# Placing stores, norm transfers and convolution tails two to four tiles later or earlier around a DeltaNet input projection

## The chip, the cores and the metric

The kernel runs on one core of one Trainium2 chip, in one launch. The metric is device time in microseconds (us); lower is better. Three runs of the kernel before gave 3073.43, 3074.57 and 3079.75 us, a median of 3074.57.

## What is computed

One inference step of a two-layer decoder for 512 prompt tokens and 8 x 4 sampled tokens, 544 in all, which share the weights. Each layer is half a feed-forward block, a token mixer, and half a feed-forward block. Layer 0 mixes by causal pooling, layer 1 by a gated DeltaNet. The change lies in the input projection of that DeltaNet:

```python
proj = h @ w_in                        # 1024 -> q, k (8 heads each), v, z (16 each), b and a
qkv, new_conv = short_conv(qkv_raw, conv_past, conv_w)   # 4 taps, then silu; also the last 3 rows
q = l2norm(q); k = l2norm(k)
o, s_new = chunk_gated_delta(q, k, v, beta, g, s0)
o = rmsnorm(o, norm_w) * silu(z)
```

`new_conv`, the last three rows before the convolution for the prompt and for each of the 8 sampled sequences, is an output of its own.

## The kernel before

All engines are programmed by hand; each runs its own list in order, and semaphores join them. Weights come in **tiles** of 128 output columns (1024 x 128, 512 KB), in two slots that take turns. For each tile SyncE (SP) issues the load into `wraw` (L400), ScalarE (ACT) rounds it into `whi` (L1039), GpSimd (POOL) makes the rest `wlo` (L545), and TensorE (PE) does 48 matmuls (L681) into one of two accumulators `acc`. SP may load a slot when POOL has read it (`w_lo`); ACT may round into a slot when PE has finished the tile two before (`acc_done`).

The input projection, `delta_in` on each engine, has 49 tiles, j = 0 to 48, written as one Python loop over j per engine: tile 0 holds b and a, tiles 1 to 16 q and k, 17 to 32 v (`V0` = 17), 33 to 48 z (`Z0` = 33). For q, k and v VectorE (DVE) scales the result into `ub` and, one tile later, adds three taps (L1653); ACT does the first tap (L1124) and the silu (L1136, L1137). A z tile is scaled by DVE (L1695) and goes through silu on ACT (L1158). The results of v and z stand in four buffers `sv` that take turns: SP stores each one to scratch memory (L452, L460 for the last two) and ACT waits for the store of four tiles before (`vz_stored`). When q and k are through (`SS_UNIT` = 18), ACT makes the inverse norms `rs16` in its iteration 19 (L1147, L1150); SP sends them to memory (L443), and reads them back spread over all partitions into `y`, four heads at a time (`norms`, L436, 1088 KB each). DVE multiplies them in, two heads per z tile (`key_norm`, L1659), and SP stores those heads (L457). Where these transfers stand between the loads is set in the SP loop by numbers alone:

```python
for j in range(IN_UNITS + 2):
    fill(j)                                  # load of tile j; 49 and 50 are the first two of w_out
    if j == SS_UNIT + 3:
        sp.wait_ge(nq_rs, 2)
        sp.dma_start(rs_d, rs16[:, 1, :]).then_inc(rs_out, 16)
...
    n = j - V0 - 4
    if 0 <= n < HV + ZT:
        sp.wait_ge(vz_silu, n + 1)
```

The convolution's rows (`tailc`) are turned by PE in eight groups of four transposes (L980), one after each tile from `TAIL_UNIT` = 41 on, and copied by DVE to `crow` (L1707, L1709). SP stores them as nine small transfers of three rows (L462, L464). The stage that follows, `delta_core`, lies over the same memory: DVE waits for all stores (`qk_stored`, `vz_stored`, `conv_stored`), clears `Y`, `S` and `gate` (L1488 to L1491), and by the last of these allows SP to load the first chunk (L491), for which PE waits (L763).

Of the kernel before, what the change touches and what calls it, by code (L numbers as in the profile page):

```python
# [8 lines left out]
SEQ, NB, NS = 512, 8, 4  # L9
# [4 lines left out]
HK, HV, DK = 8, 16, 128  # L14
CONV_DIM = 2 * HK * DK + HV * DK
CT = CONV_DIM // P
ZT = HV
CW = 4
# [21 lines left out]
CTAIL = CW - 1 + NB * NS  # L40
# [23 lines left out]
def cols(hf):  # L64
    return slice(hf * HT, (hf + 1) * HT)
# [16 lines left out]
def build(nc, consts, I, O):  # L82
# [5 lines left out]
    with ctx:  # L88
        def sb(name, shape, dt=F, scope=ctx):
            return scope.enter_context(nc.sbuf_tensor(name, shape, dt))  # L90

        def sem(name):
            return ctx.enter_context(nc.semaphore(name))
# [37 lines left out]
        aux = [ctx.enter_context(nc.psum_tensor(f"aux{b}", [P, 512], F)) for b in range(4)]  # L131
# [40 lines left out]
        vz_silu = sem("vz_silu")  # L172
        vz_stored = [sem(f"vz_stored{s}") for s in range(4)]
# [11 lines left out]
        tail_ps = sem("tail_ps")  # L185
        crow_c = sem("crow_c")
        gates_ready = sem("gates_ready")
        conv_stored = sem("conv_stored")
# [133 lines left out]
        with ExitStack() as sc:  # L322
# [4 lines left out]
            sv = [sb(f"sv{s}", [P, T], F, sc) for s in range(4)]  # L327
            sqn = sv[2:4]
            tailc = sb("tailc", [P, CT, CTAIL], F, sc)
            crow = sb("crow", [CTAIL, CONV_DIM], F, sc)  # L330
# [21 lines left out]
        v_d = nc.dram_tensor("v_scratch", [HV, P, T], F, kind="Internal").ap()  # L352
        z_d = nc.dram_tensor("z_scratch", [HV, P, T], F, kind="Internal").ap()
# [12 lines left out]
        def in_unit(j):  # L366

            return IN_BASE + j, slot(IN_BASE + j), visit(IN_BASE + j)
# [4 lines left out]

        Q0, V0, Z0 = 1, 1 + 2 * HK, 1 + CT
        SS_UNIT = Q0 + 2 * HK + 1
        TAIL_UNIT = Z0 + 8

        block = ctx.enter_context(nc.Block())

# [2 lines left out]
        def _(sp):  # L382
# [13 lines left out]
            def load(unit, i, src, nk, width=P):  # L396

                s, v = slot(unit), visit(unit)
                sp.wait_ge(w_lo[s], i + (v + 1))
                sp.dma_start(wraw[s][:, 0:nk, 0:width], src.rearrange("(k p) n -> p k n", p=P))\  # L400
                  .then_inc(raw_full[s], 16)
# [17 lines left out]
            def load_out(i, k):  # L419
                load(OUT_BASE + k, i, w_out[k * D:(k + 1) * D, bass.ds(i * P, P)] if not isinstance(i, int)  # L420
                     else w_out[k * D:(k + 1) * D, i * P:(i + 1) * P], KT)

            def delta_in():
                def fill(j):
                    if j == 0:
                        load(IN_BASE, 0, w_in[:, (CT + ZT) * P:(CT + ZT) * P + 2 * HV], KT, 2 * HV)
                    elif j < IN_UNITS:
                        load(IN_BASE + j, 0, w_in[:, (j - 1) * P:j * P], KT)
                    else:
                        load_out(0, j - IN_UNITS)  # L430

                def norms(b):
                    sp.wait_ge(rs_out, 16)
                    if b >= 2:
                        sp.wait_ge(nq_done, 4 * (b - 1))
                    sp.dma_start(y[:, 4 * (b % 2):4 * (b % 2) + 4, :], rs_d[4 * b:4 * b + 4, :].partition_broadcast(P))\  # L436
                      .then_inc(rs_in[b % 2], 16)

                for j in range(IN_UNITS + 2):
                    fill(j)  # L440
                    if j == SS_UNIT + 3:
                        sp.wait_ge(nq_rs, 2)
                        sp.dma_start(rs_d, rs16[:, 1, :]).then_inc(rs_out, 16)  # L443
                    if j == SS_UNIT + 4:
                        norms(0)
                        norms(1)
                    if j in (Z0 + 4, Z0 + 6):
                        norms((j - Z0) // 2)
                    n = j - V0 - 4
                    if 0 <= n < HV + ZT:  # L450
                        sp.wait_ge(vz_silu, n + 1)
                        sp.dma_start((v_d if n < HV else z_d)[n % HV], sv[n % 4][:, :]).then_inc(vz_stored[n % 4], 16)  # L452
                    n = j - Z0 - 3
                    if 0 <= n < HK:
                        sp.wait_ge(nq_done, 2 * n + 2)
                        for t in (2 * n, 2 * n + 1):
                            sp.dma_start(qk_d[t], qk[:, t, :]).then_inc(qk_stored, 16)  # L457
                for n in range(HV + ZT - 2, HV + ZT):
                    sp.wait_ge(vz_silu, n + 1)
                    sp.dma_start(z_d[n % HV], sv[n % 4][:, :]).then_inc(vz_stored[n % 4], 16)  # L460
                sp.wait_ge(crow_c, 8)
                sp.dma_start(O["conv_prompt"][0, 0, :, :], crow[0:CW - 1, :]).then_inc(conv_stored, 16)  # L462
                for b in range(NB):
                    sp.dma_start(O["conv_sample"][0, b, :, :], crow[CW - 1 + NS * b + 1:CW - 1 + NS * (b + 1), :])\  # L464
                      .then_inc(conv_stored, 16)
                sp.wait_ge(conv_stored, 16 * (NB + 1))

            def load_sampled(i, q):
# [201 lines left out]
        def _(pe):  # L670
# [272 lines left out]
            def delta_in():  # L943
                pre(4)
                ready = lambda hf: (h_lo, 16 * NTH[4] + 8 * (hf + 1))
                for j in range(IN_UNITS):
# [17 lines left out]
                    if 0 <= t < 2 * HK:  # L964
# [6 lines left out]
                        last.then_inc(nq_ss, 1)  # L971
                    b = j - TAIL_UNIT
                    if 0 <= b < 8:
# [318 lines left out]
        def _(dve):  # L1292
            def take(u, i, hf):

                s, v = slot(u), visit(u)
                dve.wait_ge(acc_done[s], (i + v) * 2 + hf + 1)
                return acc[s][:, hf, 0:HT]
# [86 lines left out]
            for t, n in TT:  # L1384
                for kk in range(2):
                    b = 2 * t + kk
# [216 lines left out]
            def delta_in():  # L1603
                b, a = bat[:, :, 0:HV], bat[:, :, HV:2 * HV]
# [63 lines left out]
                for j in range(IN_UNITS):  # L1668
                    u, s, v = in_unit(j)
                    if j == 0:  # L1670
                        for hf in range(2):
                            bank = take(u, 0, hf)
                            dve.tensor_tensor(ba[:, cols(hf)], bank[0:2 * HV, :], rpre[0:2 * HV, hf, :], ALU.mult).then_inc(taken[s], 1)
                    elif j < Z0:
                        c = j - Q0
                        dst = ub[c % 2]
                        samp = dst[:, CW - 1 + SEQ:UB].rearrange("p (b t) -> p b t", b=NB)
                        if c >= 2:
                            dve.wait_ge(conv_done, 3 * (c - 1))
                        dve.tensor_copy(samp[:, :, 0:CW - 1], pastc[:, c, :].rearrange("p (b t) -> p b t", b=NB))  # L1680
                        dve.tensor_tensor(dst[:, CW - 1:CW - 1 + HT], take(u, 0, 0), rpre[:, 0, :], ALU.mult).then_inc(taken[s], 1)
                        bank = take(u, 0, 1)
                        n = SEQ - HT
                        dve.tensor_tensor(dst[:, CW - 1 + HT:CW - 1 + SEQ], bank[:, 0:n], rpre[:, 1, 0:n], ALU.mult)
                        dve.tensor_tensor(samp[:, :, CW - 1:CW - 1 + NS], samples(bank[:, n:HT], 0), samples(rpre[:, 1, n:HT], 0),
                                          ALU.mult).then_inc(taken[s], 1)
                    else:
                        z = j - Z0
                        dst = conv[z % 2]
                        if z < 2:  # L1690
                            dve.wait_ge(vz_silu, HV - 1 + z) if z else dve.wait_ge(vz_silu, HV - 1)
                        else:
                            dve.wait_ge(vz_silu, HV + z - 1)
                        for hf in range(2):
                            last = dve.tensor_tensor(dst[:, cols(hf)], take(u, 0, hf), rpre[:, hf, :], ALU.mult).then_inc(taken[s], 1)  # L1695
                    if 0 <= j - Q0 - 1 < CT:
                        taps(j - Q0 - 1)
                    for m, step in ((1, gates_1), (2, gates_2), (4, gates_3), (SS_UNIT + 1, gates_4)):
                        if j == m:
                            step()  # L1700
                    if Z0 + 1 <= j <= Z0 + HK:
                        for t in range(2 * (j - Z0 - 1), 2 * (j - Z0)):
                            key_norm(t)
                    bb = j - TAIL_UNIT - 1
                    if 0 <= bb < 7:
                        dve.wait_ge(tail_ps, bb + 1)
                        dve.tensor_copy(crow[:, bb * 512:(bb + 1) * 512], aux[3 - bb % 2][0:CTAIL, :]).then_inc(crow_c, 1)  # L1707
                dve.wait_ge(tail_ps, 8)
                dve.tensor_copy(crow[:, 7 * 512:8 * 512], aux[2][0:CTAIL, :]).then_inc(crow_c, 1)  # L1709

            def pool_mixer():
                dve.memset(hp[:, :, 0:POOLP], 0.0).then_inc(hp_ready, 1)
# [81 lines left out]
            for t, n in TT:  # L1794
                for kk in range(2):
                    b = 2 * t + kk
# [56 lines left out]
```

## Time and profile before

| | |
|---|---|
| three runs | 3073.43, 3074.57, 3079.75 us |
| the profiled execution's own time | 3073.24 us |
| its span | 3071.5 us |
| mean granted TensorE clock | 0.919 of full speed |
| PE busy | 2699.7 us, 88% of the span |
| DVE, POOL, ACT busy | 1223.3, 968.3, 831.1 us |

The span runs from the first to the last instruction of the profiled execution; some 1.7 us lie around it. `delta_in` fills about 1404 to 1755 us of it, and the first matmul of `delta_core` starts at 1779.76. Matmul times in the rows are from start to a modelled end and overlap, so that the pace is read from starts and counts.

### The profile page before, as it was taken

To read this page: it belongs to the slowest core of one execution; us is meant where nothing else is said; L and a number is where in the kernel's file an instruction comes from. 1 tells how busy PE (TensorE), PEld (TensorE's weight loads), DVE (VectorE), ACT (ScalarE), POOL (GpSimd) and SP (SyncE) were. 2 spreads that over 40 slices of the span, in tenths; PEclk is the share of its full clock that TensorE was granted. 3 is DMA by queue.
4 is the path that set the end of the run, shared out by engine and by line. 5 is a ranking of instruction groups with operands and counts; after the bars stand their busy time and mean duration, and the time that the engine had idled before them with its cause. 6 is when DMAs were issued, how large, how long until landed. Compare 5 with 4: busy or idle time off the path is not lost.

```text
span 3071.5 us, 51275 instructions
## 1 busy us (share of the span) xinstructions
PE 2699.7 (88%) x20143; PEld 2580.1 (84%) x20143; DVE 1223.3 (40%) x2204; ACT 831.1 (27%) x1296; POOL 968.3 (32%) x453
## 2 busy tenths in 40 slices
PE   7999974899998999997989878989866649899997
PEld 7999972899997999996889868888754349799996
DVE  4313328531334322327776255454422342531334
ACT  4422221431323422224443211011100042441321
POOL 2333322233342333432333323132111323233432
PEclk9999987999999999998999989999955579999998
DMA  3332320132331232231246410010024323132231
GB/s 108 89 89 82 92 71 19 57 93 78 89 91 53 86 96 78 84 88 42 76 126 180 148 49 21 20 41 20 27 61 113 115 79 89 55 91 86 82 95 57
DMA packets 424267, 239.39 MB, mean 78 GB/s; under 512 B 15462, under 2 KB 411983, under 8 KB 423622
## 3 DMA queue, kind: packets, MB, share of 16 engines
q1 hardware_dynamic: 413523, 233.37, 26.0%
q10 hardware_dynamic: 10670, 5.01, 0.6%
q8 instruction: 50, 0.82, 0.1%
q14 instruction: 24, 0.20, 0.0%
HBM read 208.18 MB, written 30.52 MB: 78 GB/s over the span
## 4 chain that ended last, share of the span: by engine, by line
PE 81%; DVE 9%; DMA 3%; ACT 2%; SPq 2%; issue 1%; POOL 1%; DVEq 0%; ACTq 0%; POOLq 0%
PE acc L681 64%; PE aux L802 2%; PE aux L813 1%; PE acc L813 1%; PE acc L802 1%; DVE y L1323 1%; PE aux L817 1%; PE acc L817 1%; DVE x L1326 1%; PE aux L690 1%; PE acc L880 1%; PE aux L880 1%; DVE rpost L1301 1%; PE acc L908 1%; DMA wraw<-in_dn_w_in_dram 1%
## 5 line engine op out<-in xcount | busy, mean ns | idle before, releaser
L545 POOL TENSOR_TENSOR wlo<-wraw,whi 128x1024 fp32r<-128x1024 f32 (+2 forms) x305 | 784.8, 2574 | 1434.5 <-ACT whi L1039 1434.5
L681 PE MATMUL acc<-hhi,whi 128*128 128x272 f32 x3600 | 1042.4, 290 | 13.1 <-POOL wlo L545 13.1
L681 PE MATMUL acc<-hlo,whi 128*128 128x272 f32 x3600 | 1044.6, 290 | 0.0
L681 PE MATMUL acc<-hhi,wlo 128*128 128x272 f32 x3600 | 1037.3, 288 | 0.0
L681 PEld LDWEIGHTS acc<-hhi,whi 128*128 128x128 f32 x3600 | 678.8, 189 | 21.5 <-POOL wlo L545 13.8
L681 PEld LDWEIGHTS acc<-hhi,wlo 128*128 128x128 f32 x3600 | 679.6, 189 | 0.5
L681 PEld LDWEIGHTS acc<-hlo,whi 128*128 128x128 f32 x3600 | 677.5, 188 | 0.3
L1039 ACT ACTIVATE whi<-wraw 128x1024 fp32r<-128x1024 f32 (+2 forms) x305 | 340.0, 1115 | 407.1 <-PE acc L681 327.7
L681 PE MATMUL acc<-hidhi,whi 128*128 128x272 f32 x1408 | 406.2, 289 | 12.4 <-DVE hidlo L1348 12.4
L681 PE MATMUL acc<-hidhi,wlo 128*128 128x272 f32 x1408 | 407.6, 290 | 0.0
L681 PE MATMUL acc<-hidlo,whi 128*128 128x272 f32 x1408 | 405.0, 288 | 0.0
L681 PEld LDWEIGHTS acc<-hidhi,whi 128*128 128x128 f32 x1408 | 265.5, 189 | 14.1 <-issue 14.1
L681 PEld LDWEIGHTS acc<-hidlo,whi 128*128 128x128 f32 x1408 | 265.0, 188 | 0.0
L681 PEld LDWEIGHTS acc<-hidhi,wlo 128*128 128x128 f32 x1408 | 264.8, 188 | 0.0
L1341 DVE TENSOR_TENSOR tmpu<-acc,rpre 128x272 f32<-128x272 f32 x176 | 77.7, 441 | 344.0 <-PE acc L681 344.0
L1339 DVE TENSOR_TENSOR tmpg<-acc,rpre 128x272 f32<-128x272 f32 x176 | 77.7, 441 | 309.1 <-PE acc L681 308.1
L1080 ACT ACTIVATE hidhi<-hidf 128x272 f32 (+1 forms) x176 | 76.0, 432 | 418.9 <-DVE hidf L1345 418.9
L1345 DVE TENSOR_TENSOR hidf<-tmpu,sil 128x272 f32<-128x272 f32 x176 | 145.9, 829 | 6.0
L1653 DVE SCALAR_TENSOR_TENSOR conv<-ub,convw,conv 128x568 f32<-128x568 f32 x96 | 140.4, 1462 | 5.6 <-ACT conv L1124 3.3
L1076 ACT ACTIVATE sil<-tmpg 128x272 f32<-128x272 f32 x176 | 75.7, 431 | 225.0 <-DVE tmpg L1339 224.5
L1360 DVE COPY y<-acc 128x272 f32 x64 | 28.3, 441 | 238.9 <-PE acc L681 238.9
L1060 ACT ACTIVATE sqt<-y 128x272 f32 (+1 forms) x96 | 41.3, 431 | 296.8 <-DVE y L1362 199.2
(309 smaller groups left out, 3082.3 us busy)
## 6 DMA issues: line engine op xcount, KB each, us to landing
wraw<-in_w_ffn_gate_dram SPq DMA_DIRECT2D x88, 512.0 KB, 3.8
wraw<-in_w_ffn_up_dram SPq DMA_DIRECT2D x88, 512.0 KB, 3.8
wraw<-in_w_ffn_down_dram SPq DMA_DIRECT2D x64, 704.0 KB, 4.5
wraw<-in_dn_w_in_dram SPq DMA_DIRECT2D x48, 512.0 KB, 4.1
wraw<-in_dn_w_out_dram SPq DMA_DIRECT2D x16, 512.0 KB, 4.0
Ss<-in_state_delta_dram SPq DMA_DIRECT2D x16, 512.0 KB, 6.7
out_delta_sample_dram<-Ss SPq DMA_DIRECT2D x16, 512.0 KB, 5.9
v_scratch<-sv SPq DMA_DIRECT2D x16, 272.0 KB, 2.2
```

The lines of the kernel that those rows point to most:

```text
L545: pool.tensor_tensor(wlo[s][:, 0:nk, 0:width], wraw[s][:, 0:nk, 0:width], whi[s][:, 0:nk, 0:width].bitcast(F), ALU.subtract).then_inc(w_lo ...
L681: last = pe.matmul(acc[s][0:width, hf, 0:HT], w[s][:, k, 0:width], a[:, k0 + k, cols(hf)], start=(n == 0), stop=(n == 3 * nk - 1))
L802: last = pe.matmul(b0[0:r, heads(g, r // 2, h)].rearrange("p (b l) -> p b l", l=2 << lv), g.low[0:r, h, :], halves(g.U[0:r, h, :], lv)[:, ...
L813: last = pe.matmul(b1[0:r, heads(g, r // 2, h)].rearrange("p (b l) -> p b l", l=2 << lv), g.T[0:r, h, :], halves(g.Y[lv][0:r, h, :], lv)[: ...
L817: last = pe.matmul(b1[0:r, heads(g, r // 2, 4 + h)].rearrange("p (b l) -> p b l", l=2 << lv), g.Y[lv][0:r, h, :], halves(g.T[0:r, h, :], l ...
L1039: act.activation(whi[s][:, 0:nk, 0:width], wraw[s][:, 0:nk, 0:width], ACT.Copy).then_inc(w_hi[s], 1)
L1076: act.activation(sil[:, hf, :], tmpg[:, hf, :], ACT.Silu).then_inc(gate_silu, 1)
L1080: act.activation(hidhi[:, bass.ds(i, 1), cols(hf)], hidf[:, hf:hf + 1, :], ACT.Copy).then_inc(hid_hi, 1)
L1339: dve.tensor_tensor(tmpg[:, hf, :], take(base, i, hf), rpre[:, hf, :], ALU.mult).then_inc(taken[sg], 1)
L1341: dve.tensor_tensor(tmpu[:, hf, :], take(base + 1, i, hf), rpre[:, hf, :], ALU.mult)\
L1345: dve.tensor_tensor(hidf[:, hf, :], tmpu[:, hf, :], sil[:, hf, :], ALU.mult).then_inc(hid_ready, 1)
L1653: dve.scalar_tensor_tensor(dst[:, 0:UB - 3], src[:, k:UB - 3 + k], convw[:, CT * k + c:CT * k + c + 1], dst[:, 0:UB - 3], ALU.mult, ALU.ad ...
```

## The change

In SP's loop the store of v or z tile n moves from j = V0 + n + 4 to V0 + n + 6; the norms' store from j = 21 to 24; the first two transfers back from 22 to 26, the others from 37 and 39 to 40 and 42; the q/k stores begin at j = 39 instead of 36. The last four z stores, not two, stand behind the loop. PE's tail transposes and DVE's copies begin at tile 34 (`TAIL_UNIT` = Z0 + 1) instead of 41, so that the last copy stands in the loop too, and the nine convolution stores are issued at j = 47, in front of the loads of tiles 48 to 50. No operation is added or taken away.

```diff
-        TAIL_UNIT = Z0 + 8
+        TAIL_UNIT = Z0 + 1
...
+                def store_vz(n):
+                    sp.wait_ge(vz_silu, n + 1)
+                    sp.dma_start((v_d if n < HV else z_d)[n % HV], sv[n % 4][:, :]).then_inc(vz_stored[n % 4], 16)
...
-                    if j == SS_UNIT + 3:
+                    if j == SS_UNIT + 6:
                         sp.wait_ge(nq_rs, 2)
                         sp.dma_start(rs_d, rs16[:, 1, :]).then_inc(rs_out, 16)
-                    if j == SS_UNIT + 4:
+                    if j == SS_UNIT + 8:
                         norms(0)
                         norms(1)
-                    if j in (Z0 + 4, Z0 + 6):
-                        norms((j - Z0) // 2)
-                    n = j - V0 - 4
+                    if j in (Z0 + 7, Z0 + 9):
+                        norms((j - Z0 - 3) // 2)
+                    n = j - V0 - 6
                     if 0 <= n < HV + ZT:
-                        sp.wait_ge(vz_silu, n + 1)
-                        sp.dma_start((v_d if n < HV else z_d)[n % HV], sv[n % 4][:, :]).then_inc(vz_stored[n % 4], 16)
-                    n = j - Z0 - 3
+                        store_vz(n)
+                    n = j - Z0 - 6
...
-                sp.wait_ge(crow_c, 8)
-                sp.dma_start(O["conv_prompt"][0, 0, :, :], crow[0:CW - 1, :]).then_inc(conv_stored, 16)
...
+                    if j == TAIL_UNIT + 13:
+                        sp.wait_ge(crow_c, 8)
+                        sp.dma_start(O["conv_prompt"][0, 0, :, :], crow[0:CW - 1, :]).then_inc(conv_stored, 16)
...
+                for n in range(HV + ZT - 4, HV + ZT):
+                    store_vz(n)
                 sp.wait_ge(conv_stored, 16 * (NB + 1))
```

SP's queue where the v tiles begin, before; the first row is the load of tile 21, and the wait in brackets is what SP must have before it issues the row:

```order
L400 DMA wraw<-in_dn_w_in_dram 128x8x128 [waits w_lo1]
L443 DMA rs_scratch<-rs 16x544 [waits nq_rs]
L452 DMA v_scratch<-sv 128x544 [waits vz_silu]
L400 DMA wraw<-in_dn_w_in_dram 128x8x128 [waits w_lo0]
L436 DMA y<-rs_scratch 128x2176 [waits rs_out] x2
L452 DMA v_scratch<-sv 128x544 [waits vz_silu]
```

And now, from the load of tile 24 to behind that of tile 26:

```order
L400 DMA wraw<-in_dn_w_in_dram 128x8x128 [waits w_lo0]
L447 DMA rs_scratch<-rs 16x544 [waits nq_rs]
L434 DMA v_scratch<-sv 128x544 [waits vz_silu]
L400 DMA wraw<-in_dn_w_in_dram 128x8x128 [waits w_lo1]
L434 DMA v_scratch<-sv 128x544 [waits vz_silu]
L400 DMA wraw<-in_dn_w_in_dram 128x8x128 [waits w_lo0]
L440 DMA y<-rs_scratch 128x2176 [waits rs_out] x2
L434 DMA v_scratch<-sv 128x544 [waits vz_silu]
```

The norms' store has moved behind three more loads, and the two transfers of the norms behind four more.

SP's queue where `delta_in` ends, before; the first row is the load of tile 48:

```order
L400 DMA wraw<-in_dn_w_in_dram 128x8x128 [waits w_lo0]
L452 DMA z_scratch<-sv 128x544 [waits vz_silu]
L400 DMA wraw<-in_dn_w_out_dram 128x8x128 [waits w_lo1]
L452 DMA z_scratch<-sv 128x544 [waits vz_silu]
L400 DMA wraw<-in_dn_w_out_dram 128x8x128 [waits w_lo0]
L452 DMA z_scratch<-sv 128x544 [waits vz_silu]
L460 DMA z_scratch<-sv 128x544 [waits vz_silu] x2
L462 DMA out_conv_prompt_dram<-crow 3x4096 [waits crow_c]
L464 DMA out_conv_sample_dram<-crow 3x4096 x8
L483 UNCONDITIONAL_BRANCH [waits vz_stored1,vz_stored2,vz_stored0,vz_stored3,qk_stored,conv_stored]
```

And now, from the load of tile 47:

```order
L400 DMA wraw<-in_dn_w_in_dram 128x8x128 [waits w_lo1]
L434 DMA z_scratch<-sv 128x544 [waits vz_silu]
L463 DMA out_conv_prompt_dram<-crow 3x4096 [waits crow_c]
L465 DMA out_conv_sample_dram<-crow 3x4096 x8
L400 DMA wraw<-in_dn_w_in_dram 128x8x128 [waits w_lo0]
L434 DMA z_scratch<-sv 128x544 [waits vz_silu]
L400 DMA wraw<-in_dn_w_out_dram 128x8x128 [waits w_lo1]
L434 DMA z_scratch<-sv 128x544 [waits vz_silu]
L400 DMA wraw<-in_dn_w_out_dram 128x8x128 [waits w_lo0]
L434 DMA z_scratch<-sv 128x544 [waits vz_silu] x5
L486 UNCONDITIONAL_BRANCH [waits vz_stored1,vz_stored2,vz_stored0,vz_stored3,qk_stored,conv_stored]
```

The nine convolution stores have moved from the end of the queue to in front of the load of the last z tile, and five z stores stand behind the last load.

## Rows read from the trace of the kernel before

**Rows 1.** The page, share of the chain that ended last, by engine.

```profile
PE 81%; DVE 9%; DMA 3%; ACT 2%; SPq 2%; issue 1%; POOL 1%; DVEq 0%; ACTq 0%; POOLq 0%
```

**Rows 2.** Busy time by stretch: PE, PEld, DVE, ACT, POOL, then PEclk, DMA, GB/s.

```profile
1600.00:1620.00 20.00, 20.00 (x162) 20.00 (x161) 18.34 (x23) 8.06 (x18) 8.19 (x4) 1.00 0.48 137
...
1680.00:1700.00 20.00, 19.22 (x135) 19.22 (x136) 4.74 (x9) 4.82 (x6) 8.20 (x4) 0.86 0.72 226
...
1759.00:1761.00 2.00, 0.00 (x0) 0.00 (x0) 0.00 (x0) 0.00 (x0) 0.00 (x0) 0.50 0.13 33
```

**Rows 3.** The chain that ended last, in order of time: start, us, what.

```profile
1550.80 6.24 PE acc L681 x48
...
1570.29 11.13 DMA wraw<-in_dn_w_in_dram
1582.59 2.40 POOL wlo L545
1585.03 78.80 PE acc L681 x624
...
1680.78 26.59 PE acc L681 x192
1707.37 0.44 PE aux L980 x4
...
1762.31 4.07 DMA out_conv_sample_dram<-crow
```

**Rows 4.** Timeline of PE: start, us, what, [idle before <- releaser].

```profile
1576.72 0.59 PE L681 MATMUL acc<-hhi,whi 128*128 128x272 f32 x1 [7.62 <-POOL wlo L545]
...
1680.78 0.60 PE L681 MATMUL acc<-hhi,whi 128*128 128x272 f32 x1 [4.89 <-POOL wlo L545]
...
1779.76 1.22 PE L763 MATMUL acc<-kT 128*128 128x128 f32 x4 [26.64 <-DMA vT<-v_scratch]
```

**Rows 5.** What SP's queue waited for, 1390 to 1800: us, times, longest.

```profile
SPq L443 <- ACT rs L1150: 20.5, 1, 20.5
SPq L457 <- DVE qk L1659: 20.4, 5, 7.0
...
SPq L491 <- DVE gate L1491: 8.7, 1, 8.7
```

**Rows 6.** Timeline of ACT in its iterations 19 and 20.

```profile
1557.12 1.06 ACT L1039 ACTIVATE whi<-wraw 128x1024 fp32r<-128x1024 f32 x1 [1.48 <-PE acc L681]
...
1566.36 0.66 ACT L1150 ACTIVATE rs<-rs 16x544 f32<-16x544 f32 x1
...
1567.09 0.25 ACT L1153 ACTIVATE gtmp<-gates 128x80 f32<-128x80 f32 x1
1573.19 1.06 ACT L1039 ACTIVATE whi<-wraw 128x1024 fp32r<-128x1024 f32 x1 [5.85 <-DMA wraw<-in_dn_w_in_dram]
```

**Rows 7.** Timeline of DVE: two sets of taps, and the first clearing.

```profile
1557.48 4.62 DVE L1653 SCALAR_TENSOR_TENSOR conv<-ub,convw,conv 128x568 f32<-128x568 f32 x3
...
1568.38 2.49 DVE L1653 SCALAR_TENSOR_TENSOR conv<-ub,convw,conv 128x568 f32<-128x568 f32 x3
...
1766.64 6.43 DVE L1488 MEMSET Y<- 128x512 f32 x12 [12.28 <-DMA out_conv_sample_dram<-crow]
```

**Rows 8.** Timeline of POOL: the split of tile 22, and the idle time before it.

```profile
1574.32 2.34 POOL L545 TENSOR_TENSOR wlo<-wraw,whi 128x1024 fp32r<-128x1024 f32 x1 [13.67 <-ACT whi L1039]
```

**Rows 9.** Line L460, the last two z stores: issue ns, starts; time to landing.

```profile
L460 SPq DMA_DIRECT2D z_scratch<-sv x2: 319/319/319, 1747.9 to 1754.4; - x2
...
DMA to landing us min/median/max: 2.0/2.0/2.0
```

**Rows 10.** Line L452, the other stores of v and z: time to landing.

```profile
DMA to landing us min/median/max: 2.0/4.5/10.4
```

**Rows 11.** The page, DMA issues: KB each, median us to landing.

```profile
wraw<-in_dn_w_in_dram SPq DMA_DIRECT2D x48, 512.0 KB, 4.1
```

**Rows 12.** Timeline of SP: the eight convolution stores of the samples.

```profile
1755.13 7.75 SPq L464 DMA_DIRECT2D out_conv_sample_dram<-crow x8
```

More of the change, by code:

```diff
@@ L457, in delta_in @@
                             sp.dma_start(qk_d[t], qk[:, t, :]).then_inc(qk_stored, 16)
-                for n in range(HV + ZT - 2, HV + ZT):
-                    sp.wait_ge(vz_silu, n + 1)
-                    sp.dma_start(z_d[n % HV], sv[n % 4][:, :]).then_inc(vz_stored[n % 4], 16)
-                sp.wait_ge(crow_c, 8)
-                sp.dma_start(O["conv_prompt"][0, 0, :, :], crow[0:CW - 1, :]).then_inc(conv_stored, 16)
-                for b in range(NB):
-                    sp.dma_start(O["conv_sample"][0, b, :, :], crow[CW - 1 + NS * b + 1:CW - 1 + NS * (b + 1), :])\
-                      .then_inc(conv_stored, 16)
+                    if j == TAIL_UNIT + 13:
+                        sp.wait_ge(crow_c, 8)
+                        sp.dma_start(O["conv_prompt"][0, 0, :, :], crow[0:CW - 1, :]).then_inc(conv_stored, 16)
+                        for b in range(NB):
+                            sp.dma_start(O["conv_sample"][0, b, :, :], crow[CW - 1 + NS * b + 1:CW - 1 + NS * (b + 1), :])\
+                              .then_inc(conv_stored, 16)
+                for n in range(HV + ZT - 4, HV + ZT):
+                    store_vz(n)
                 sp.wait_ge(conv_stored, 16 * (NB + 1))
@@ L1704, in delta_in @@
                     bb = j - TAIL_UNIT - 1
-                    if 0 <= bb < 7:
+                    if 0 <= bb < 8:
                         dve.wait_ge(tail_ps, bb + 1)
                         dve.tensor_copy(crow[:, bb * 512:(bb + 1) * 512], aux[3 - bb % 2][0:CTAIL, :]).then_inc(crow_c, 1)
-                dve.wait_ge(tail_ps, 8)
-                dve.tensor_copy(crow[:, 7 * 512:8 * 512], aux[2][0:CTAIL, :]).then_inc(crow_c, 1)
             def pool_mixer():
```

## The prediction

> **What bounds the kernel now.** I read the chain that ended last first: 81% of it is on TensorE [rows 1], so time is won only where PE stands still or runs slowly. The stretches of `delta_in` say where. From 1600 to 1620 PE issues 162 matmuls in 20 us at full clock [rows 2], and the chain shows the pace behind that: tiles 23 to 35, 624 matmuls, in 78.80 us, which is 6.06 us a tile [rows 3]. Nothing moved by the change can beat that pace. So I looked for PE's gaps, and its timeline has three: 7.62, 4.89 and 26.64 us [rows 4]. Behind each gap stands SP's queue. SP waited 20.5 us in one piece for the norms (L443) and 20.4 us in five for `key_norm` (L457) [rows 5]. While SP waits, the loads behind it in its list are not issued.
>
> *First gap.* The norms are ready at 1566.36 + 0.66 = 1567.0 [rows 6]. SP, which has issued tile 21, waits until then and only then loads tile 22. ACT was free at 1567.34 but gets the weights at 1573.19 [rows 6]. The load of tile 23 stands behind two 1088 KB transfers and takes 11.13 us [rows 3]. PE had ended tile 21 at 1576.72 - 7.62 = 1569.10 [rows 4]. At 6.06 a tile it would have begun tile 23 at 1575.1 and begins it at 1585.03 [rows 3]: 9.9 us lost.
>
> *Second gap.* Tiles 38 to 41 take 26.59 us instead of 24.24 [rows 3]; the mean granted clock is 0.86 from 1680 to 1700 [rows 2], so some of them ran at the lower of its levels, 1.2 GHz. With the gap of 4.89 [rows 4] that is 7.2 us lost.
>
> *Third gap.* PE ends at 1753.12. The last z store is issued at 1754.4 and lands 2.0 us later [rows 9]. But DVE starts to clear at 1766.64, released by the convolution stores, which are issued over 7.75 us behind it [rows 7, 12], the last landing 4.07 us after its issue [rows 3]. SP waits 8.7 us for DVE's clearing [rows 5], then come the loads.
>
> **The change, part by part.**
>
> *Norms and v stores later.* At j = 24 SP has the slot of tile 24 only after POOL has split tile 22, which is after ACT's norms, so the wait is empty. Tiles 22 and 23 are loaded in time. What remains is ACT's own lateness: it is busy until 1567.34, rounds tile 22 in 1.06 us [rows 6], POOL splits in 2.40 [rows 3], and with 0.1 between them PE starts at 1570.9, 1.8 us late. Then DVE's taps for the next silu run beside that split. Taps that ran beside a split took 4.62 us, and those at 1568.38, when POOL had been idle since 1560.65, took 2.49 [rows 7, 8]. With 4.62 the silu ends near 1573.9, tile 23 is split by 1577.4, and PE, which would want it at 1576.9, loses 0.5 more. In the Trainium skill, SBUF — State Buffer, section "SBUF: two separate sides", a VectorE operation with two SBUF inputs and a GpSimd one that reads SBUF exclude each other; the trace agrees (4.62 against 2.49), and without that exclusion the rest would be 1.8 instead of 2.3 us. I take 2.3: a gain of 9.9 - 2.3 = **7.6**. It can't pass 8.1, since ACT isn't free sooner; if ACT needs two more tiles to catch up at 1.3 each, it is 5.
>
> *Norms, z stores and q/k stores later.* The q/k store at j needs `key_norm` of tile j - 5, while SP arrives when POOL has split tile j - 2, which needs the end of tile j - 4 on PE. The waits of L457 (and of the norms in front) are then empty, and loads go out 3.6 us after PE ends a tile (1.06 + 2.40 and 0.1), two tiles ahead of need. Gain **7.2**; at worst 0, if bytes and not waits hold the loads. The slowest load seen, 11.13 us behind twice as many norms, would still land 14.8 us after that tile's end; rounding and splitting need 3.6 more, and PE needs the result at 18.2. So I expect none of the 7.2 to stay. DVE may wait a little for the third norm transfer; PE asks for that only a tile later.
>
> *Tails earlier.* Eight groups of transposes of 0.44 us [rows 3] stand in PE's list as before. Seven lay between tiles, the eighth behind the last; now all lie between: **0.4** lost. DVE is busy 4.74 of 20 us in that stretch [rows 2] and hides the copies; beyond that cover, PE would wait for `crow`.
>
> *Convolution stores earlier.* Their cost moves into SP's queue at j = 47. SP gets there 3.6 us after PE ends tile 43, issues the load and a z store (about 0.8), then the nine for 8.1. The load of tile 48 goes out 12.5 us after that end instead of 9.7. It must have landed by 18.2 + 2.5 = 20.7 (2.5 is what splitting in 3.6 leaves of a tile), 8.2 us after issue. These stores keep few DMA engines busy, 0.13 of 16, or two [rows 2], so the load's shares on those queue up. A load lands in 4.1 us in the median [rows 11]; I add 2 for that queue and take **0**. With the 11.13 us of the worst load it would be 2.9 late, and the lower clock would add some 2.4 as in the second gap: 5.
>
> In the Trainium skill, DMA: Bandwidth & Descriptors, section "Why a DMA increments its semaphore by 16 and not by 1", a transfer is spread over as many engines, up to 16, as divide the slowest dimension: three for rows of 3 x 4096, the lowest-numbered each time. The trace's 0.13 agrees with two or three. This speaks against the new place, since a weight load uses all 16 and lands with its slowest share.
>
> *End.* With the convolution stores done, DVE waits for the last z store: 1754.4 + 2.0 and the same 0.25 that lay between landing and clearing before, 1756.65 instead of 1766.64: **10.0** gained. The clearing and the first loads follow unchanged, and PE's clock, down at 0.50 (1.2 GHz) from 1759 to 1761 [rows 2], is down at either time. If that store landed only after 10.4, the slowest of L452 [rows 10], the gain would be 1.6.
>
> *Sum.* 7.6 + 7.2 - 0.4 - 0 + 10.0 = 24.4 us off the profiled execution's own 3073.24: 3048.8. It lies 1.3 below the median of the runs shown; I say **3049**. The terms' bounds give 5 to 8.1, 0 to 7.2, -5 to 0 and 1.6 to 10.0.
>
> **Rivals.**
>
> *The stores at j = 47 hold up the last tile.* For it: few engines, and the load behind them. Against it: 8.2 us of room. Price 5: **3054**.
>
> *The last store lands late.* Five z stores now stand behind the last loads. Against it: four of them have time to drain while PE works on tile 48, and the two of L460 landed in 2.0 [rows 9]. Price 8.4: **3057**.
>
> *The gaps only move.* If bytes, not SP's waits, starve the loads, both gaps come back where the norms stand now, and only the end is won: **3063**. The 11.13 us load speaks for it, the 20.5 us in which SP issued nothing speak against it. Were the end's gain gone too, nothing would be left: about 3073.
>
> *Slower: the ring of four `sv` buffers.* A z store is now issued about 4.4 us after the end of the second tile following, and ACT needs it 1.1 us after the end of the fourth: 8.8 us to land. ACT is busy 4.82 of 20 us [rows 2], 1.5 a tile, so 4.5 more are spare, and splitting has 2.5: PE stalls once stores take 15.8 us. To be slower by 6 it must lose 30.5 over 16 tiles, 1.9 each, that is 17.7 us a store; at 18 it would be 35 - 24.4 above before: **3084**. L452's landings, 4.5 median and 10.4 at worst [rows 10], are far from it.
>
> **How the numbers follow.** My forecast, 3044 to 3055 with its own bounds: 0.73. Last tile held up 0.08, last store late 0.06, gaps only move 0.06, nothing left 0.03, ring 0.04. A measurement of this kernel can tell 0.2%, 6.1 us, from no change. All but the last two are faster by more than that: 0.93; same 0.03; slower 0.04. The range 3043 to 3059 takes in the forecast and the first two rivals, 0.87 together, with 1 us below and 2 above.
>
> **What would show it.** In the profile after, SP's waits for the norms' store and for `key_norm` should be near nothing. PE's gap at the start of v should be 1.8 us and one of about 0.5 behind it, with the clock up; no gap between tiles 33 and 48; the convolution stores' issue should end before the last tiles, and DVE's clearing should be released by a z store, about 4 us after PE's last tile. PE's long gap should be 16 to 17 us. A wait of ACT for the last weights, or for `vz_stored`, that reaches PE would make me wrong, as would gaps of several us two to four tiles later.

## The result and the profile after

The changed kernel takes 3051.97 us in the median of four runs (3050.74 to 3053.83), the kernel before 3077.16 in four runs beside it: a ratio of 0.9918, 95% interval 0.9900 to 0.9935. In five later runs it was 3050.81 against 3073.01, 0.9925 (0.9911 to 0.9938). It is faster by some 0.8%, 22 to 25 us by the medians. The profiled execution took 3050.74 us, its span is 3049.0. One run of the third experiment below, 3140.3 us at a granted clock of 0.841, is slow and stands in none of the numbers.

The chain of the changed kernel that ended last, in order of time (start, us, what; lines are 3 higher than before), answers to [rows 3]:

```profile
1551.03 6.24 PE acc L684 x48
...
1578.08 72.72 PE acc L684 x576
...
1690.08 6.04 PE acc L684 x48
...
1696.56 42.28 PE acc L684 x336
1740.55 2.03 DMA z_scratch<-sv
...
1752.81 2.99 DMA vT<-v_scratch
1756.02 1.22 PE acc L766 x4
```

The end of tile 48 in the kernel before, for the comparison:

```profile
1746.65 6.06 PE acc L681 x48
```

No load of weights is in this piece of the chain any more, and the link between PE's last tile and the next stage is a z store, not a convolution store. Three stretches can be measured by the same marks in both traces: from the start of tile 19 to that of tile 23 (34.23 us before, 27.05 now), from there to the end of tile 48 (1746.65 + 6.06 before; 167.68 and 160.76 us), and from there to the first matmul of `delta_core` (27.05 and 17.18). The gains are 7.18, 6.92 and 9.87 us, 23.97 together. Tile 19 itself starts 0.23 later, and the span is 22.5 shorter, so that 1.2 of the 23.7 us at the first matmul of `delta_core` is gone by the end of the program. Nothing in the change lies there, and no run shows its cause.

PE's timeline shows what is left of the gaps of [rows 4]:

```profile
1571.01 0.39 PE L684 MATMUL acc<-hhi,whi 128*128 128x272 f32 x1 [1.68 <-POOL wlo L548]
...
1578.08 0.39 PE L684 MATMUL acc<-hhi,whi 128*128 128x272 f32 x1 [0.77 <-POOL wlo L548]
...
1756.02 1.22 PE L766 MATMUL acc<-kT 128*128 128x128 f32 x4 [17.19 <-DMA vT<-v_scratch]
```

The waits of SP's queue, to be read beside [rows 5]:

```profile
SPq L400 <- POOL wlo L548: 287.3, 47, 30.1
SPq L494 <- DVE gate L1494: 8.8, 1, 8.8
SPq L434 <- ACT sv L1161: 7.2, 2, 5.7
SPq L485 <- DMA z_scratch<-sv: 1.6, 1, 1.6
SPq L434 <- ACT sv L1140: 1.0, 1, 1.0
```

The 20.5 us for the norms and the 20.4 for `key_norm` are gone. What SP waits for now is the slot of the next load (L400), which is its task. Two of the last z stores wait for silu behind the last load, where they hold up no weights, and one v store waits 1.0 us.

Busy time by stretch (PE, PEld, DVE, ACT, POOL, PEclk, DMA share, GB/s):

```profile
1560.00:1580.00 20.00, 17.55 (x138) 17.12 (x137) 14.48 (x22) 12.28 (x23) 6.20 (x3) 1.00 0.30 87
...
1660.00:1680.00 20.00, 20.00 (x163) 19.96 (x162) 8.23 (x15) 4.83 (x6) 8.86 (x4) 1.00 0.75 245
1680.00:1700.00 20.00, 20.00 (x163) 19.96 (x162) 8.54 (x16) 4.86 (x6) 8.84 (x4) 1.00 0.85 276
```

The z tiles run without a gap, with the granted clock at its upper level of 2.4 GHz, while the DMA engines are busier than before (0.85 from 1680 to 1700, against 0.72 in [rows 2]). The short gaps at 1571.01 and 1578.08 left the clock up, 1.00 from 1560 to 1580. In the kernel before the same stretch, with the gap of 7.62 us [rows 4], had 0.83:

```profile
1560.00:1580.00 20.00, 12.38 (x88) 12.16 (x87) 10.34 (x18) 9.11 (x16) 3.00 (x2) 0.83 0.56 194
```

### The profile page after: what moved, and what is told of

Read it like the earlier page. It is cut to its first block, busy times and chain, and to the rows that moved or that the text cites. A ratio compares the mean times of both kernels' runs of the same rounds, so it can differ in the third digit from the quotient of the medians.

```text
span 3049.0 us, 51275 instructions
## 1 busy us (share of the span) xinstructions
PE 2700.5 (89%) x20143; PEld 2581.6 (85%) x20143; DVE 1225.6 (40%) x2204; ACT 831.0 (27%) x1296; POOL 971.8 (32%) x453
## 4 chain that ended last, share of the span: by engine, by line
PE 82%; DVE 9%; DMA 3%; ACT 2%; issue 1%; SPq 1%; POOL 1%; DVEq 0%; ACTq 0%; POOLq 0%
PE acc L684 64%; PE aux L805 2%; PE aux L816 1%; PE acc L816 1%; PE acc L805 1%; DVE y L1326 1%; PE aux L820 1%; PE acc L820 1%; PE aux L693 1%; DVE x L1329 1%; PE acc L883 1%; PE aux L883 1%; DVE rpost L1304 1%; PE acc L911 1%; DMA out_delta_sample_dram<-Ss 1%
## 5 line engine op out<-in xcount | busy, mean ns | idle before, releaser
L1042 ACT ACTIVATE whi<-wraw 128x1024 fp32r<-128x1024 f32 (+2 forms) x305 | 340.0, 1115 | 387.5 <-PE acc L684 350.1
```

The costliest lines, as they stand in the source:

```text
L1042: act.activation(whi[s][:, 0:nk, 0:width], wraw[s][:, 0:nk, 0:width], ACT.Copy).then_inc(w_hi[s], 1)
```

## The experiments

All ran beside the kernel before, and each ratio is to that.

**Only the norms' store and the first two transfers**

```diff
-                    if j == SS_UNIT + 3:
+                    if j == SS_UNIT + 6:
...
-                    if j == SS_UNIT + 4:
+                    if j == SS_UNIT + 8:
```

> Only the norms' store (j = 24) and the first two norm transfers (j = 26) are moved; all else as before. If SP's wait at L443 starves the loads (my theory): PE's 7.62 us gap shrinks to 1.8 and a second of about 0.5, some 7.2 us faster than before (the first gap's share of the two traces: 1585.03 to 1578.08, plus 0.23 of an earlier start); the gap of 4.89 us in the z tiles and the 26.64 us at the end stay. If the bytes of the norm transfers starve the loads (rival): a gap of several us comes back about tile 27 or 28, and the time stays within 2 us of before.

Measured: 3066.82 against 3074.39, ratio 0.9973 (0.9963 to 0.9983). PE's timeline:

```profile
1571.61 0.39 PE L681 MATMUL acc<-hhi,whi 128*128 128x272 f32 x1 [1.67 <-POOL wlo L545]
...
1674.37 0.60 PE L681 MATMUL acc<-hhi,whi 128*128 128x272 f32 x1 [4.85 <-POOL wlo L545]
```

The first gap is 1.67 us with one of 0.76 behind it at tile 23, as in the changed kernel, the gap in the z tiles is 4.85 as before, and none came up between. The norm transfers move the same bytes, only four tiles later, and cost nothing there: the slowest weight load from 1560 to 1600 takes 7.7 us to land, and PE has no gap behind it. That speaks for the wait in SP's list as the cause. Wait and transfers were moved together, so that their shares in the old gap are not told apart.

**Only the stores and the last two transfers**

```diff
-                    if j in (Z0 + 4, Z0 + 6):
-                        norms((j - Z0) // 2)
-                    n = j - V0 - 4
+                    if j in (Z0 + 7, Z0 + 9):
+                        norms((j - Z0 - 3) // 2)
+                    n = j - V0 - 6
...
-                    n = j - Z0 - 3
+                    n = j - Z0 - 6
...
-                for n in range(HV + ZT - 2, HV + ZT):
+                for n in range(HV + ZT - 4, HV + ZT):
```

> Only the v, z and q/k stores and the last two norm transfers are moved; the norms' store and the first two transfers, the tails and the convolution stores stay as before. Theory: the 4.89 us gap in the z tiles and the 2.35 us at the lower clock behind it vanish, some 7 us faster than before, the 7.62 us gap at the start of v stays. Rival (bytes, not waits, hold the loads): a gap of 3 to 5 us appears somewhere in tiles 38 to 44 and the time is within 2 us of before.

Measured: 3068.09 against 3074.39, ratio 0.9977 (0.9968 to 0.9986). A row of the chain:

```profile
1586.47 115.02 PE acc L681 x912
```

912 matmuls are tiles 23 to 41 in one piece, at 6.05 us a tile: the gap in the z tiles is gone. At the start of v a gap of 5.94 us stayed.

**Only the tails and the convolution stores**

```diff
-        TAIL_UNIT = Z0 + 8
+        TAIL_UNIT = Z0 + 1
...
+                    if j == TAIL_UNIT + 13:
+                        sp.wait_ge(crow_c, 8)
+                        sp.dma_start(O["conv_prompt"][0, 0, :, :], crow[0:CW - 1, :]).then_inc(conv_stored, 16)
```

> Only the tails begin at tile 34 and the nine convolution stores stand at j = 47; stores and norms as before. Theory: DVE's clearing is released by the last z store, PE's last gap falls from 26.64 to about 17 us, some 9.6 us faster than before (10.0 at the end, 0.4 for the eighth group of transposes); the other two gaps stay. Rival: the stores at j = 47 hold up the load of tile 48 because SP's z stores are nearer now than in the change, PE waits for it some us, and 5 us or less are gained.

The tails begin seven tiles earlier, at 34 instead of 41; the two to four of the title hold for the stores and transfers.

Measured: 3063.36 against 3074.39, ratio 0.9962 (0.9950 to 0.9975). What PE waited for from 1400 to 1850 (us, times, longest):

```profile
PE acc L764 <- DMA vT<-v_scratch: 17.3, 1, 17.3
...
PE acc L682 <- POOL wlo L546: 11.7, 3, 7.1
```

The end is as in the changed kernel, 17.3 us, and the waits for weights stay (7.12, 1.04 and 3.56 us at tiles 22, 23 and in z). The three parts alone gain 7.6, 6.3 and 11.0 us by their medians, 24.9 in sum. That agrees with the 22 to 25 of the whole, within intervals of some 3 us for each part.

**The stores one tile and two tiles later still**

```diff
-                    n = j - V0 - 6
+                    n = j - V0 - 7
...
-                for n in range(HV + ZT - 4, HV + ZT):
+                for n in range(HV + ZT - 5, HV + ZT):
```

and the same with 8 and 6.

> The changed kernel with every v and z store one tile later still (n = j - V0 - 7). My sum gave ACT 8.8 us from a z store's issue to its need in the change; here 2.7 are left. With landings of 2 to 4.5 us ACT waits up to 2 us a z tile, of 4.5 spare: theory says no gap on PE in the z tiles and a time within 0.1% of the changed kernel, 0.992 of before. Rival (the ring is already close to holding up ACT): PE stalls in the z tiles and 5 us or more of the gain are lost.

> The changed kernel with every v and z store two tiles later still (n = j - V0 - 8). Now a z store is issued only behind the split that follows the rounding in ACT's same iteration, and ACT's silu waits for its landing: a tile takes rounding and splitting 3.6, issue 0.8, landing 2 to 4.5, silu 0.6, in all 7.0 to 9.5 us instead of 6.06. Over 16 z tiles, less some slack: 12 to 50 us slower than the changed kernel, near before or slower. Rival (the stores' place doesn't matter, only that SP doesn't wait): no change from the changed kernel.

Measured: one tile later 3051.15 against 3079.0, ratio 0.9915 (0.9898 to 0.9933), the same as the changed kernel; two later 3109.08, ratio 1.0098 (1.0077 to 1.0120), some 58 us above it and slower than before, beyond the 12 to 50 I expected. Waits in the z tiles, first of the kernel with the stores one tile later (1640 to 1745):

```profile
ACT sv L1161 <- DMA z_scratch<-sv: 37.8, 11, 7.7
ACT whi L1042 <- PE acc L684: 20.9, 11, 3.2
...
ACT sv L1161 <- DMA v_scratch<-sv: 5.7, 3, 2.3
```

then of that with two (1690 to 1790):

```profile
ACT sv L1161 <- DMA z_scratch<-sv: 75.5, 9, 11.4
...
PE acc L684 <- POOL wlo L548: 28.9, 10, 6.6
```

and of the changed kernel (1640 to 1745):

```profile
ACT whi L1042 <- PE acc L684: 60.5, 14, 4.9
```

In the first, ACT waits 43.5 us in 14 tiles for its buffers, 3.1 on average and 7.7 at most, where I had expected up to 2. PE has no gap all the same: ACT's waits for PE before it rounds (L1042) are 20.9 us instead of 60.5, so that its spare time takes it all. In the second the store stands in the way of every tile. A piece of its chain:

```profile
1730.47 4.72 DMA z_scratch<-sv
1735.32 0.52 issue
1735.84 1.06 ACT whi L1042
1736.96 2.35 POOL wlo L548
1739.33 0.39 SPq L400
1739.76 4.82 DMA z_scratch<-sv
```

The store lands, ACT does silu and rounds, POOL splits, SP issues the next load and then the next store. This round takes 9.3 us, against PE's 6.06 a tile, and PE is not in it. The term I had too low was the landing: 4.7 to 7.8 us from 1690 to 1790, where I had put 2 to 4.5. In the changed kernel itself no wait of ACT for a store is listed. So the ring of four buffers is the bound that the place of the stores runs into, two tiles behind the changed kernel.

**Nine more three-row stores at j = 47**

```diff
                               .then_inc(conv_stored, 16)
+                        for b in range(NB + 1):
+                            sp.dma_start(more_d[b], crow[CW - 1 + NS * (b % NB) + 1:CW - 1 + NS * (b % NB + 1), :])\
+                              .then_inc(conv_stored, 16)
```

> The changed kernel with nine more three-row stores of the same rows to scratch memory behind the nine at j = 47. In the change they take 8.1 us of SP's queue and the load of tile 48 is issued 12.5 us after PE ends tile 43, with landing allowed 8.2 us later. Twice as many: issue at about 21, landing at 25 to 26 instead of 20.7 at the latest: PE stalls 5 us before tile 48, with the lower clock behind it perhaps 7, and the time is 5 to 7 us above the changed kernel. If the stores cost more than their issue (rival: weights' shares stuck behind them on the same few DMA engines), 10 us or more.

Measured: 3061.18 against 3079.0, ratio 0.9943 (0.9927 to 0.9960); the kernel with the stores one tile later, on the same chip and without the nine, took 3051.15. So they cost 10 us. SP's timeline:

```profile
1713.94 7.88 SPq L466 DMA_DIRECT2D out_conv_sample_dram<-crow x8
1721.86 9.36 SPq L469 DMA_DIRECT2D more_scratch<-crow x9
1731.26 1.36 SPq L401 DMA_DIRECT2D wraw<-in_dn_w_in_dram x1
```

and PE's:

```profile
1741.43 0.59 PE L688 MATMUL acc<-hhi,whi 128*128 128x272 f32 x1 [8.48 <-POOL wlo L552]
```

and two rows of the chain:

```profile
1731.26 6.60 DMA wraw<-in_dn_w_in_dram
...
1741.43 8.32 PE acc L688 x48
```

The load goes out 22.5 us after PE ends tile 43 (1696.72 + 12.08), not 21, and lands 6.60 later, so that PE waits 8.48; tile 48 then takes 8.32 instead of 6.06, part of it with the clock down (0.75 from 1742 to 1750). The gap and that are 10.7 us, where I gave 5 to 7. Beside the changed kernel, whose load of tile 48 goes out 12.8 us after that end and lands some 6.0 later, the issue is 9.6 us later and the landing 0.6 slower; less 1.9 us of slack, that is the gap. So it has the form I expected, an issue too late. My size was too small by the 1.0 us that each three-row store holds SP, where I had 0.9, and by a landing of 4 to 5. Both loads are slower than the median of 4.4 in the changed kernel from 1560 to 1745; whether they waited for the stores on the same DMA engines, as in my rival, is neither shown nor excluded.

**The changed kernel once more, and tile 22 rounded ahead of the norms**

```diff
                 for j in range(IN_UNITS):
-                    round_weights(IN_BASE + j + 2)
+                    if j != SS_UNIT + 2:
+                        round_weights(IN_BASE + j + 2)
...
                     if j == SS_UNIT + 1:
+                        round_weights(IN_BASE + j + 3)
                         act.wait_ge(nq_ss, 2 * HK)
```

> The changed kernel as it is, to stand on the same chip beside the next three: 0.992 of before, as measured.

> The changed kernel, with ACT rounding tile 22 in its iteration 19 ahead of the norms instead of behind them. Theory: the 1.8 us that PE still waits before tile 22 is ACT's lateness, so PE's gap there vanishes, and the time is about 1.5 us below the changed kernel; the 0.5 before tile 23, which hangs on DVE's taps, may stay. Rival (DVE's late taking of the accumulator holds PE): the gap stays at 1 us or more.

Measured: the changed kernel 3050.81, ratio 0.9925 (0.9911 to 0.9938); with tile 22 first 3049.89, 0.9925 (0.9912 to 0.9939): no difference that can be told. PE's timeline of the latter:

```profile
1568.86 0.36 PE L684 MATMUL acc<-hhi,whi 128*128 128x272 f32 x1 [0.42 <-DVE ub L1686]
...
1576.34 0.39 PE L684 MATMUL acc<-hhi,whi 128*128 128x272 f32 x1 [1.21 <-POOL wlo L548]
```

The wait before tile 22 fell from 1.68 to 0.42, as ACT's lateness would have it, but that before tile 23 rose from 0.77 to 1.21. From tile 19 to tile 23 it is 26.21 instead of 27.05 us. My forecast of 1.5 was too high: ACT's work on the norms is no shorter, DVE waits for it with the next accumulator, and the silu and the rounding behind that are late by themselves.

**Clearing ahead of the last z store**

```diff
-                dve.wait_ge(qk_stored, 16 * 2 * HK)
-                for s in range(4):
-                    dve.wait_ge(vz_stored[s], 16 * 8)
-                dve.wait_ge(conv_stored, 16 * (NB + 1))
-                for q in range(2):
-                    for n in range(LEVELS):
-                        dve.memset(GP[q].Y[n][:], 0.0)
                 dve.memset(S[:], 0.0)
+                for s in range(4):
+                    dve.wait_ge(vz_stored[s], 16 * 8)
...
+                    if j in (IN_UNITS - 2, IN_UNITS - 1):
+                        q = j - (IN_UNITS - 2)
+                        dve.wait_ge(qk_stored, 16 * 2 * HK)
+                        if q == 1:
+                            dve.wait_ge(conv_stored, 16 * (NB + 1))
+                        for n in range(LEVELS):
+                            dve.memset(GP[q].Y[n][:], 0.0)
```

> The changed kernel, with DVE clearing Y inside the last two z tiles and S before it waits for the last z store. Theory: the end is now bound by the last z store's landing and then 8.2 us of clearing; with the clearing out of the way SP's first loads go out some 8.8 us sooner, PE's last gap falls from 17.2 to about 8.5 us, 0.989 of before. Rival: the clearing holds up DVE's taking of tiles 47 and 48 or POOL's splits, and 3 us or more of that are given back.

> Both of the two before in one kernel: the sum of their gains, about 10 us below the changed kernel, 0.9885 of before, if they are independent.

Measured: 3043.27 against 3073.01, ratio 0.9899 (0.9884 to 0.9914); with tile 22 first as well 3046.65, 0.9909 (0.9896 to 0.9923), which is no better, so that the sum I expected of the two is not shown. 7.5 us are gained over the changed kernel, where I had expected 8.8. PE's long gap and DVE's timeline say why:

```profile
1748.38 1.22 PE L766 MATMUL acc<-kT 128*128 128x128 f32 x4 [10.44 <-DMA vT<-v_scratch]
```

```profile
1738.47 3.19 DVE L1708 MEMSET Y<- 128x512 f32 x6
1742.03 1.76 DVE L1485 MEMSET S<- 128x2048 f32 x1 [0.38 <-DMA z_scratch<-sv]
```

The second half of `Y` begins only after tile 48 is taken and ends at 1741.66, just as the last z store lands. By the edit `S` waits for no store any more, though the row names one, but it still comes behind that landing, because `Y` is late. So the halves were moved one tile ahead (IN_UNITS - 3 and IN_UNITS - 2):

> clear_early once more, with the two halves of Y cleared in tiles 46 and 47 instead of 47 and 48. There the second half was cleared only after tile 48 had been taken, so that S (1.76 us) still lay behind the last z store's landing and SP's first load went out 7.7 us sooner instead of 8.8. Theory: now only the two gate clearings lie behind the landing, PE's last gap falls from 10.4 to about 8.6 us, and the time is some 1.8 us below clear_early, 0.9893 of before. Rival: the loads of the first chunk are late for another reason, and the gap stays at 10.4.

> clear_earlier with tile 22 rounded ahead of the norms as in round_first: 0.8 us less in the trace before tile 23, as round_first showed; in the time no difference from clear_earlier that this measurement can tell.

Measured: 3041.15 against 3073.41, ratio 0.9893 (0.9876 to 0.9909); with tile 22 first 3041.45, 0.9897 (0.9880 to 0.9913). DVE's timeline of the former:

```profile
1739.42 1.76 DVE L1485 MEMSET S<- 128x2048 f32 x1 [0.37 <-issue]
1742.48 0.11 DVE L1489 MEMSET gate<- 128x20 f32 x2 [1.29 <-DMA z_scratch<-sv]
```

and PE's:

```profile
1747.10 1.22 PE L766 MATMUL acc<-kT 128*128 128x128 f32 x4 [8.53 <-DMA vT<-v_scratch]
```

DVE is through and waits for the store, and PE's gap is 8.53 us, as expected. The step from 0.9899 to 0.9893 is smaller than the intervals, so that only the gap shows it. Against the kernel before, this version and the one ahead of it gain more than the change (0.9925 in its own batch).

## Why the prediction was right

3049 us were forecast, in a range of 3043 to 3059; the medians are 3051.97 and 3050.81.

*Start of v.* Forecast 7.6, found 7.18. The rest was to be 1.8 and 0.5; the gaps are 1.68 and 0.77. Of the 9.9 us lost before, some 1.4 were tile 22 itself, which took 7.70 us from its start to its end, with the clock down behind the long gap, and takes 6.30 now. The sum holds them without naming them; they are won because the clock stayed up, which the prediction has among its signs. ACT rounds tile 22 as soon as the norms are done, and DVE's taps beside that split took 4.65 us:

```profile
1568.61 4.65 DVE L1656 SCALAR_TENSOR_TENSOR conv<-ub,convw,conv 128x568 f32<-128x568 f32 x3
```

Before, with POOL idle, the set at this place took 2.49 [rows 7]. With tile 22 rounded ahead of the norms, POOL is through sooner and the same set takes 2.49 again. The exclusion that the Trainium skill states (SBUF — State Buffer, "SBUF: two separate sides") is what these three traces look like; they do not show that the port is its cause. It goes both ways, which the sum left out: beside the next taps the split of tile 23 took 2.96 us instead of 2.40, which alone makes up for 0.77 in place of 0.5.

```profile
1575.07 2.96 POOL L548 TENSOR_TENSOR wlo<-wraw,whi 128x1024 fp32r<-128x1024 f32 x1 [4.11 <-ACT whi L1042]
```

*Tiles of z.* Forecast 7.2 - 0.4, found 6.92 over tiles 23 to 48. Of the three parts only the second experiment has no such gap, so it is the stores' and transfers' places, not the tails.

*Convolution stores at j = 47.* Forecast 0, with the load of tile 48 issued 12.5 us after the end of tile 43 and landing some 6 later. SP and ACT of the changed kernel:

```profile
1713.70 7.74 SPq L465 DMA_DIRECT2D out_conv_sample_dram<-crow x8
1721.48 1.04 SPq L400 DMA_DIRECT2D wraw<-in_dn_w_in_dram x1
...
1727.47 1.06 ACT L1042 ACTIVATE whi<-wraw 128x1024 fp32r<-128x1024 f32 x1 [5.06 <-DMA wraw<-in_dn_w_in_dram]
```

It goes out 12.8 us after that end (1696.56 + 12.08 = 1708.64), and ACT has it 18.8 after it, where 20.7 were allowed. PE does not notice, but only 1.9 us were left, and nine stores more cost 10.

*End.* Forecast 10.0, found 9.87: DVE's clearing is released by the z store, 1742.94 instead of 1766.64, that is 4.1 us behind PE's last tile instead of 13.5, and the 8.7 us of clearing stay:

```profile
1742.94 6.43 DVE L1491 MEMSET Y<- 128x512 f32 x12 [3.63 <-DMA z_scratch<-sv]
```

PE's gap of 17.19 lies just over the 16 to 17 that were named, since the eighth group of transposes (0.44) no longer stands at its start.

*Rivals.* That the gaps only move is refuted by the first two experiments. That the last store lands late is not what happened: it landed in 2.03 us. The ring of `sv` holds: the z stores landed in 2.0 to 8.3 us, where the sum allowed 8.8 before ACT waits. The two kernels with later stores show where it ends. The bound of 15.8 us for PE was not reached at this place, so that no run tests it.

## What to carry to other kernels

A queue that is served in order should not wait for a late producer while loads stand behind it: read the queue's own waits first, and move the waiting transfer back until its wait is empty, here two to four places, with no byte saved. The way back is bounded by the buffers that the store frees: count from its new place to the next use of its buffer, and set the spare time of the engines between against it; here one place more was free and two more cost 58 us. Small stores at the end of a stage belong ahead of the last loads only as far as the loads have slack, and clearing for the next stage belongs ahead of the last store it does not depend on.

## What the runs showed of the hardware that was not expected

A store of three rows of 16 KB held SP's queue for about 1 us on average where it followed others of its kind, 7.74 to 7.88 for eight (some 0.3 for the first) and 9.36 for nine more. A store of 544 columns of 128 rows (272 KB, more than five times the bytes) took 0.58 us to issue in the median in the changed kernel, with 0.32 to 3.24 as its bounds. So the issue time did not go by bytes here. Why it takes that long was not tried, and that SP was held by what already stood in the queue is not excluded.
